# Hybrid encoder block on one core: first norm and w_in in two halves, the last modulation column in the V pass, the query weight loaded by k tile

## The chip, the core and the metric

The kernel runs on one core of a Trainium2 chip. Its engines are TensorE (PE: matmuls; PEld is its weight load), VectorE (DVE), ScalarE (ACT) and GpSimd (POOL). SyncE (SP) issues most of the loads. The metric is the time of one execution in microseconds, as the device measures it. All data are float32 in HBM.

## The reference

```python
c_act = jax.nn.silu(c)
mod = c_act @ ada_w[l] + ada_b[l]                 # 2048 x 12288 weight: 100 MB
shift1, scale1, gate1, shift2, scale2, gate2 = jnp.split(mod, 6, axis=-1)
h = modulate(rms_norm(x, pre_mix_g[l]), shift1, scale1)
proj = h @ w_in[l]                                # 2048 -> 1856: pool | q latent | kv latent | rope key
y_pool = multiscale_pool(proj[..., :o1], pool_w[l], pool_scale[l])
y_mla = mla_attention(proj[..., o1:o2], ...)      # 8 heads, low-rank q and kv, rotary part
y = jnp.concatenate([y_pool, y_mla], axis=-1) @ w_out[l]
x = x + gate1[:, None, :] * rms_norm(y, post_mix_g[l])
h = modulate(rms_norm(x, pre_ffn_g[l]), shift2, scale2)
y = peer_ffn(h, peer_wq[l], peer_sub_keys[l], peer_u[l], peer_v[l])   # 16384 experts
x = x + gate2[:, None, :] * rms_norm(y, post_ffn_g[l])
```

Sequence 256, model width 2048, one layer.

## The kernel before

**Stages.** The program is written out by hand, engine by engine, with semaphores between them. In order of time: the first norm and its modulation (0 to 111 us), w_in (to 202), the latent projections and the pooling mixer (to 256), attention over 8 heads (to 315), w_out (to 412), second norm, the query weight wq (443 to 551), all 16384 experts' u rows (128 tiles, to 1316), a scatter of the gates (to 1430), all v rows (128 tiles, to 2130), and the tail.

**Float32 products.** Each large product is made of three matmuls of a rounded high part and a low part (the three lines of `split3`, L591 to L593). ACT rounds a weight pair (two k tiles) to `win_high`, `wout_high` or `wq_high` (`weight_high`, L937), DVE makes the low part in place (`weight_low`, L1237). `win_high` has three buffers, so ACT and DVE are at most three pairs ahead of PE. The weights w_uq, w_ukv and pool_w are used as plain float32 (L586).

**The modulation** is no matmul over 2048 but a sum on DVE. `ada_w` is cut into six parts of 2048 columns; a part comes in 8 pieces of 2 MB, and DVE takes 4 steps for a piece: `acc = piece * c_act[:, k] + acc` over 1024 columns (L1227 for the first, L1229 for the others; `ada(n)` is n such steps, 32 to a part). After 32 steps `ada_columns` on PE sums over the partitions into a column of `ps` (L568, 32 instructions), and `scale_column`, `shift_column` or `gate_column` finish it. Gates also go through `gate_rows` (PE), `gate_out` (ACT) and a store to DRAM, from which GpSimd loads them as rows. Steps stand in DVE's queue wherever the author put them, between the other work; a step waits for its piece.

**The ring.** Weights and pieces share six slots of 2 MB, filled by SP strictly in the order of `load_order()`. A load waits until the one six places before it is released:

```python
if kind == "ada":
    return ada_op, i * STEPS + 4 * h + 4
if kind in WEIGHTS:
    return w_used, pair_no(kind, i, 4 * h + 3) + 1
return {"uq": (qpe_mm, 2), "ukv": (v_mm, 4), "pool": (pool_mm, 8), "keys": (key_mm, 4)}[kind]
```

So a piece is released by DVE's fourth step on it, a weight block by PE's last pair of it, the two halves of w_uq by the second rope-query group (`qpe_mm`), w_ukv by the last value group (`v_mm` 4), and pool_w by the last pooling group (`pool_mm` 8).

**Between w_in and attention.** PE makes the queries and the rope queries from the latents `cT`, then the keys, then for each of four pooling groups g two products that wait for `z_ready` g+1 (DVE's `pool_group(g)`, running sums over `uT`), then the values, then it transposes the rotated queries (`k_roped`, `q_roped` from DVE's `rotate`). The first score matmuls follow, and DVE's `maxima(0)` (L1413) opens the softmax chain of the heads.

**u and v passes.** In a v tile ACT rounds two halves of 128x1024 (L1175), DVE makes their low parts (L1667), PE multiplies.

## Time and profile before

| | |
|---|---|
| time, median of 3 runs | 2152.22 us (2151.8 to 2155.94) |
| the profiled execution's own time | 2155.08 us |
| its span, first to last instruction | 2152.3 us |
| PE busy / DVE busy | 1946.9 us (90%) / 1520.1 us (71%) |
| mean granted TensorE clock | 0.96 |
| chain that ended last: PE / DVE / DMA / issue | 79% / 10% / 3% / 3% |

The span is shorter than the time by 2.8 us, which lies before the first and behind the last instruction. PE carries most of the chain that ended last, but not in the first 111 us, where it is busy for 23.7 us.

### The profile page before, as it was taken

The page shows a single profiled execution, that of the slowest core. Times are in us where ns is not written, and L with a number is a line of the kernel's source. Part 1 is how long each engine was busy: PE and PEld are TensorE (multiplying, and loading weights), DVE is VectorE, ACT ScalarE, POOL GpSimd, SP SyncE. Part 2 cuts the span into 40 slices and gives each one's busy share as a digit, 9 for nine tenths or more (in the row PEclk, how much of TensorE's full clock was granted, in tenths as well). Part 3 has the DMA queues.
Part 4 walks back from the last instruction along what each step waited for, and adds up shares of the span by engine and source line. Part 5 has one row for each costly group of instructions (what it writes and reads, how often), then busy time and mean ns, then how long its engine had stood idle before and what let it go on. Part 6 is the DMA issues. An engine that isn't in the chain of part 4 may idle for free.

```text
span 2152.3 us, 37807 instructions
## 1 busy us (share of the span) xinstructions
PE 1946.9 (90%) x12388; PEld 1757.5 (82%) x12388; DVE 1520.1 (71%) x2136; ACT 898.1 (42%) x1311; POOL 432.6 (20%) x290
## 2 busy tenths in 40 slices
PE   0489989798999999999999997679999999999995
PEld 0479658698999999999999997568888888888884
DVE  6897489775689999999976667975555555555554
ACT  1143233453334444444444445654444444444443
POOL 1000020000234444444444446840000000000001
PEclk9799859899999999999999999999999999999998
DMA  9989469979567676666677771045555555555553
GB/s 392 414 306 353 157 246 367 295 227 268 131 168 183 180 184 182 180 182 176 175 186 180 184 183 59 0 134 192 192 194 195 194 190 192 194 195 192 190 193 117
DMA packets 227889, 436.99 MB, mean 203 GB/s; under 512 B 23106, under 2 KB 157696, under 8 KB 214016
## 3 DMA queue, kind: packets, MB, share of 16 engines
q1 hardware_dynamic: 226240, 427.84, 63.9%
q0 software_dynamic: 1536, 8.48, 1.0%
q8 instruction: 30, 0.49, 0.1%
q14 instruction: 19, 0.16, 0.0%
q10 hardware_dynamic: 64, 0.02, 0.0%
HBM read 432.04 MB, written 4.21 MB: 203 GB/s over the span
## 4 chain that ended last, share of the span: by engine, by line
PE 79%; DVE 10%; DMA 3%; issue 3%; ACT 2%; DVEq 1%; SPq 1%; POOL 0%; ACTq 0%; POOLq 0%
PE ps L591 14%; PE ps L592 14%; PE ps L593 14%; PE ps L877 11%; PE ps L878 11%; PE ps L880 11%; DVE acc L1229 3%; DVE hotB L1636 2%; DMA ring<-in_ada_w_dram 2%; PE ps L586 2%; DMA i<-consts_dram 1%; DVEq L1636 1%; DVE ring_low L1237 1%; PE ps L568 1%; PE ps L703 1%
## 5 line engine op out<-in xcount | busy, mean ns | idle before, releaser
L591 PE MATMUL ps<-h2H,eH 128*128 128x256 f32 x2048 | 581.5, 284 | 5.8 <-DVE eL L1584 4.5
L592 PE MATMUL ps<-h2L,eH 128*128 128x256 f32 x2048 | 581.0, 284 | 0.0
L593 PE MATMUL ps<-h2H,eL 128*128 128x256 f32 x2048 | 580.9, 284 | 0.0
L1667 DVE TENSOR_TENSOR eL<-raw,eH 128x1024 fp32r<-128x1024 f32 x256 | 313.6, 1225 | 338.2 <-ACT eH L1175 338.2
L1175 ACT CAST eH<-raw 128x1024 fp32r<-128x1024 f32 x256 | 269.9, 1055 | 385.4 <-PE ps L880 379.8
L496 POOL TENSOR_TENSOR eL<-raw,eH 128x1024 fp32r<-128x1024 f32 x128 | 311.4, 2433 | 572.9 <-ACT eH L1101 572.9
L877 PE MATMUL ps<-eH,aH 128*128 128x512 f32 x1024 | 399.2, 390 | 3.6 <-DVE eL L1667 3.6
L591 PEld LDWEIGHTS ps<-h2H,eH 128*128 128x128 f32 x2048 | 394.6, 193 | 6.7 <-DVE eL L1584 5.2
L878 PE MATMUL ps<-eL,aH 128*128 128x512 f32 x1024 | 398.9, 390 | 0.0
L593 PEld LDWEIGHTS ps<-h2H,eL 128*128 128x128 f32 x2048 | 394.7, 193 | 0.0
L592 PEld LDWEIGHTS ps<-h2L,eH 128*128 128x128 f32 x2048 | 394.6, 193 | 0.0
L1593 DVE STREAM_TRANSPOSE raw<-raw 128x1024 f32<-128x1024 f32 x256 | 317.4, 1243 | 87.2 <-DMA raw<-in_peer_u_dram 79.0
L1101 ACT CAST eH<-raw 128x1024 fp32r<-128x1024 f32 x256 | 267.2, 1045 | 199.6 <-PE ps L593 160.1
L880 PE MATMUL ps<-eH,aL 128*128 128x512 f32 x1024 | 315.7, 389 | 0.0
L1229 DVE SCALAR_TENSOR_TENSOR acc<-ring,c_act,acc 128x1024 f32<-128x1024 f32 x180 | 227.1, 1295 | 23.1 <-DMA ring<-in_ada_w_dram 20.9
L877 PEld LDWEIGHTS ps<-eH,aH 128*128 128x128 f32 x1024 | 192.7, 188 | 43.8 <-issue 3.7
L880 PEld LDWEIGHTS ps<-eH,aL 128*128 128x128 f32 x1024 | 192.5, 188 | 40.1
L878 PEld LDWEIGHTS ps<-eL,aH 128*128 128x128 f32 x1024 | 192.6, 188 | 39.9
L1584 DVE TENSOR_TENSOR eL<-raw,eH 128x1024 fp32r<-128x1024 f32 x128 | 155.9, 1218 | 39.1 <-ACT eH L1101 38.5
L350 POOL TENSOR_TENSOR result<-x,scaled 128x2048 f32<-128x2048 f32 x1 | 4.5, 4474 | 712.7 <-DVEq L1687 712.7
L1116 ACT ACTIVATE acts<-ps 128x256 f32 (+1 forms) x128 | 49.2, 384 | 225.0 <-PE ps L593 225.0
L591 PE MATMUL ps<-h2H,wq_high 128*128 128x256 f32 x256 | 76.2, 297 | 13.6 <-DVE ring_low L1237 11.5
(254 smaller groups left out, 2313.1 us busy)
## 6 DMA issues: line engine op xcount, KB each, us to landing
raw<-in_peer_u_dram SPq DMA_DIRECT2D x1024, 128.0 KB, 3.0
raw<-in_peer_v_dram SPq DMA_DIRECT2D x256, 512.0 KB, 3.4
ring<-in_ada_w_dram SPq DMA_DIRECT2D x48, 2048.0 KB, 19.9
ring<-in_w_out_dram SPq DMA_DIRECT2D x8, 2048.0 KB, 11.9
ring<-in_peer_wq_dram SPq DMA_DIRECT2D x32, 512.0 KB, 15.5
ring<-in_w_in_dram SPq DMA_DIRECT2D x6, 2048.0 KB, 14.7
ring<-in_w_uq_dram SPq DMA_DIRECT2D x2, 1536.0 KB, 9.0
ring<-in_w_in_dram SPq DMA_DIRECT2D x2, 1280.0 KB, 11.7
```

Of the source, the lines that this page charges most:

```text
L496: pool.tensor_tensor(by_k(eL[:, j % RING, :]), turned(raw[:, j % RAW, :]), by_k(eH[:, j % RING, :].bitcast(F32)), ALU.subtract).then_inc(u ...
L591: pe.matmul(o, lh, rh, start=start, stop=False, skip_group_check=True)
L592: pe.matmul(o, lh, rl, start=False, stop=False, skip_group_check=True)
L593: return pe.matmul(o, ll, rh, start=False, stop=stop, skip_group_check=True)
L877: pe.matmul(o[n], lh, vh[n], start=start, stop=False, skip_group_check=True)
L878: pe.matmul(o[n], lh, vl[n], start=False, stop=False, skip_group_check=True)
L880: mm = pe.matmul(o[n], ll, vh[n], start=False, stop=stop, skip_group_check=True)
L1101: act.copy(by_k(eH[:, j % RING, :]), turned(raw[:, j % RAW, :])).then_inc(u_hi, 1)
L1175: act.copy(eH[:, slot, :], raw[:, slot, :]).then_inc(v_hi, 1)
L1229: ins = dve.scalar_tensor_tensor(a, w, c_act[:, k:k + 1], a, ALU.mult, ALU.add)
L1593: dve.transpose(raw[:, j % RAW, :], raw[:, j % RAW, :]).then_inc(u_tr, 1)
L1667: dve.tensor_tensor(eL[:, slot, :], raw[:, slot, :], eH[:, slot, :].bitcast(F32), ALU.subtract).then_inc(v_lo, 1)
```

## The change

1. **Modulation parts 0 and 1** are cut another way: part 0 is now the first 1024 columns of shift1 and of scale1 together, part 1 the second 1024 of both. A piece of them comes in two loads of 1 MB. The first norm's modulation and w_in are done in two halves of 8 k tiles: PE runs the low half of all four column blocks n = 2, 3, 0, 1, with `ada_columns(1)` ahead of the last of them, then the high half of all four. x is loaded after the first piece, and the constants from ACT's queue.
2. **Positions of steps.** DVE takes 34 steps ahead of the first modulation (64 before), then 30 in the low half, 12 in the high half, 28 between w_in and attention (6 before), 18 in attention as before, 38 in w_out (40), none in wq (32).
3. **The rope angles** (`angles()`) move from the start to the last column block of w_in's high half, ahead of the diagonal matrices `diag` and `tmpr` that PE's latent transposes wait for (`lat_diag`).
4. **Gate 1:** `ada_columns(2)` and `gate_rows(0)` move from the projections to the start of w_out.
5. **Gate 2** (part 5, 16.8 MB) leaves the ring and the wq stage. It comes as 16 pieces of 1 MB in the v pass, the first three from SP, the others from GpSimd's queue; DVE takes one step a tile in tiles 3 to 34, then a transpose, a reduction and two row operations. `ada_columns(5)`, `gate_rows(1)` and `gate_out(1)` around the first u round are gone.
6. **wq** is loaded with 8 loads of 256 KB over 128 partitions for a block, before with 4 loads of 512 KB over 32 partitions each.

```diff
-PARTS = (1, 0, 2, 3, 4, 5)
+PARTS = (None, None, 2, 3, 4, 5)
...
-    win = [("win", n, h) for n in WIN_ORDER for h in range(2)]
     wout = [("wout", n, h) for n in range(4) for h in range(2)]
     wq = [("wq", n, h) for n in range(4) for h in range(2)]
-    between = ([("uq", 0, 0), ("ada", 3, 0), ("uq", 1, 0), ("ada", 3, 1), ("ukv", 0, 0), ("pool", 0, 0)]
-               + [("ada", 3, p) for p in range(2, PIECES)])
-    return ([("ada", 0, p) for p in range(PIECES)] + [("ada", 1, p) for p in range(PIECES)] + mixed(win, 2)
-            + between + mixed(wout, 4) + mixed(wq, 5) + [("keys", 0, 0)])
+    low, step = [], 0
+    for n, count in zip(WIN_ORDER, (3, 3, 1, 1)):
+        low += [("win", n, 0)] + [("ada", 1, step + p) for p in range(count)]
+        step += count
+    high = [("win", n, 1) for n in WIN_ORDER]
+    between = ([("ada", 2, 0), ("ada", 2, 1), ("uq", 0, 0), ("ada", 2, 2), ("uq", 1, 0), ("ada", 2, 3), ("ukv", 0, 0),
+                ("pool", 0, 0)] + [("ada", 2, p) for p in range(4, PIECES)] + [("ada", 3, p) for p in range(PIECES)])
+    return ([("ada", 0, p) for p in range(PIECES)] + low + high
+            + between + mixed(wout, 4) + wq + [("keys", 0, 0)])
...
-        per_slot[n % SLOTS] += 64 if key[0] == "wq" else 16
+        per_slot[n % SLOTS] += 128 if key[0] == "wq" else 32 if key[0] == "ada" and key[1] < 2 else 16
...
+        def load_piece(eng, k):
+            eng.dma_start(piece[k % 3][:], ada_v[:, k, 5 * D:6 * D]).then_inc(piece_done(k)[0], 16)
...
+                if kind == "ada" and i < 2:
+                    for k in range(2):
+                        sp.dma_start(dst[:, k * D:(k + 1) * D].rearrange("p (m n) -> p m n", m=2),
+                                     ada_v[:, 2 * h + k, 0:2 * D].rearrange("p (m n) -> p m n", m=2)
+                                     [:, :, i * 1024:(i + 1) * 1024]).then_inc(done, 16)
+                elif kind == "ada":
...
-                    for q in range(4):
-                        sp.dma_start(wide(kind, i, 8 * h)[q * QUAD:(q + 1) * QUAD],
-                                     wq_v[q, :, ks, i * W:(i + 1) * W]).then_inc(done, 16)
+                    for k in range(8):
+                        sp.dma_start(wide(kind, i, 8 * h)[:, k, :],
+                                     wq_v[8 * h + k, :, :, i * W:(i + 1) * W]).then_inc(done, 16)
...
+            sp.wait_ge(u_used, 2 * TILES)
+            for k in range(3):
+                load_piece(sp, k)
...
+            for k in range(3, KT):
+                pool.wait_ge(piece_step, 2 * (k - 2))
+                load_piece(pool, k)
...
-            ada_columns(1, 0)
-
-
-            for n in WIN_ORDER:
-                if n == 1:
-                    pe.wait_ge(lat_out, 2)
-                for k in range(KT):
-                    if n == 2 and k % 2 == 0:
+            ada_columns(0, 0, 0)
+
+            def win_half(n, half):
+
...
+            for n in (2, 3, 0):
+                win_half(n, 0)
+            ada_columns(1, 7, HI_COLS, False)
+            win_half(1, 0)
+
+
+            for n in WIN_ORDER:
+                win_half(n, 1)
                 if n == 0:
                     pe.wait_ge(lat_diag, 4)
...
-            pe.wait_ge(u_out, 8)
             for tt in range(TT):
                 mm_group(ps[:, 4 + tt, :], lambda k: cT[:, k, tt * P:(tt + 1) * P],
                          lambda k: wuq[k // 2][:, k % 2, :, NOPE:NOPE + ROPE], 4).then_inc(qpe_mm, 1)
-            ada_columns(2, 0)
...
-            gate_rows(0, 1)
-
             pe.wait_ge(k_roped, 1)
             pe.wait_ge(q_roped, 1)
-            pe.wait_ge(grow_out, 1)
+            pe.wait_ge(u_out, 8)
...
+            ada_columns(2, 0, 2 * KT)
             for n in range(4):
                 for k in range(KT):
+                    if n == 0 and k == 8:
+                        gate_rows(0, 1)
...
-            ada_columns(5, 3)
             for i in range(ROUND):
                 u_tile(0, i, i < 3)
-            gate_rows(1, 3)
...
-            gate_out(1, 3)
...
+            def input_columns(i, bank, first):
+
+                dve.wait_ge(acc_used, 2 * i + 2)
+                cols = slice(8 * i, 8 * i + 8)
+                dve.tensor_tensor(mod1[:, 1, cols], ps[:, bank, first:first + 8], vcols[:, V_B0 + 8 * i:V_B0 + 8 * i + 8],
+                                  ALU.add)
+                seq(dve.scalar_tensor_tensor(mod1[:, 0, cols], ps[:, bank, first + 8:first + 16], 1.0,
+                                             vcols[:, V_B1 + 8 * i:V_B1 + 8 * i + 8], ALU.add, ALU.add))
+                dve.nop().then_inc(mod_read, 1)
+                seq(dve.tensor_tensor(mod1[:, 0, cols], mod1[:, 0, cols], vcols[:, V_G1 + 8 * i:V_G1 + 8 * i + 8], ALU.mult))
...
+            def inputs(half):
+
+                k0 = 8 * half
+                for k in range(k0, k0 + 4):
+                    modulate(k)
+                if half:
+                    weight_low("win", 1, 2)
+                h_low(k0 // 2)
+                modulate(k0 + 4)
+                modulate(k0 + 5)
+                if half:
+                    weight_low("win", 1, 3)
+                else:
+                    weight_low("win", 2, 0)
+                h_low(k0 // 2 + 1)
+                modulate(k0 + 6)
+                modulate(k0 + 7)
+                h_low(k0 // 2 + 2)
+                weight_low("win", 2, 4 if half else 1)
+                h_low(k0 // 2 + 3)
...
+            ada(10)
...
+            ada(18)
+            ada(2)
+            input_columns(0, 0, 0)
             dve.wait_ge(xn_out, KT)
-
-            def modulate(k):
-                dve.tensor_scalar(hT[:, k, :], hT[:, k, :], mod1[:, 0, k:k + 1], mod1[:, 1, k:k + 1],
-                                  ALU.mult, ALU.add).then_inc(h_f, 1)
-
-            def h_low(j):
-                dve.wait_ge(h_hi, j + 1)
-                h = slice(2 * j, 2 * j + 2)
-                dve.tensor_tensor(hL[:, h, :], hT[:, h, :], hH[:, h, :].bitcast(F32), ALU.subtract).then_inc(h_lo, 1)
-
-            for k in range(4):
-                modulate(k)
-            for j in range(2, KT // 2):
-                modulate(2 * j)
-                modulate(2 * j + 1)
-                h_low(j - 2)
-                if j == 3:
-                    weight_low("win", 2, 0)
-            h_low(KT // 2 - 2)
-            weight_low("win", 2, 1)
-            h_low(KT // 2 - 1)
-
+            inputs(0)
             for n in WIN_ORDER:
-                for j in range(8):
-                    if n == 0 and j == 5:
+                for j in range(4):
+                    if (n, j) in ((2, 0), (2, 1), (1, 2), (1, 3)):
+                        continue
+                    weight_low("win", n, j)
+                    ada({2: 2, 3: 3, 0: 3, 1: 1}[n])
+            input_columns(1, 7, HI_COLS)
+            inputs(1)
+            for n in WIN_ORDER:
+                for j in range(4, 8):
+                    if n != 2 or j >= 5:
+                        weight_low("win", n, j)
+                    if n == 0 and j == 7:
...
+                    if n == 1 and j == 5:
                         dve.wait_ge(lat_sq, 3)
...
-                    ada(1)
-            dve.wait_ge(trig_ready, 2)
-
+                    if n < 2:
+                        ada(2 - n)
+                    if n == 1 and j == 4:
+                        angles()
...
+            ada(6)
+            dve.wait_ge(trig_ready, 2)
...
+            ada(4)
...
-            gate_column(0, 2, 0, V_B2, V_PO1)
-            ada(6)
+            ada(18)
...
-                    ada(2 if j % 4 == 3 else 1)
+                    ada(2 if j == 3 or (n < 2 and j == 7) else 1)
+                    if n == 0 and j == 2:
+                        gate_column(0, 2, 0, V_B2, V_PO1)
...
-                    ada(1)
...
-            gate_column(1, 5, 3, V_B5, V_PO2)
...
-            with dve.Fori(1, TILES // 3) as r:
+            def last_gate(step):
+
+                k, h = step // 2, step % 2
+                if h == 0:
+                    dve.wait_ge(*piece_done(k))
+                a, w = (t[:, h * 1024:(h + 1) * 1024] for t in (sums2, piece[k % 3]))
+                if k == 0:
+                    dve.tensor_scalar(a, w, c_act[:, 0:1], None, ALU.mult).then_inc(piece_step, 1)
+                else:
+                    dve.wait_ge(piece_step, step - 1)
+                    dve.scalar_tensor_tensor(a, w, c_act[:, k:k + 1], a, ALU.mult, ALU.add).then_inc(piece_step, 1)
+
+            def gate_row(i, op):
+                dve.wait_ge(gate2_in, 16)
+                dve.wait_ge(extra_in, 16 * (i + 1))
+                dve.tensor_tensor(gate2[:], gate2[:], extra[:], op).then_inc(gate2_ready, 1)
+
+            for tile in range(3, 36):
+                v_tile(tile, tile % 3, False)
+                if tile < 35:
+                    last_gate(tile - 3)
+            dve.wait_ge(piece_step, 2 * KT)
+            dve.transpose(sums2[:], sums2[:]).then_inc(sums_turned, 1)
```

How the change moves instructions is shown at three places. First SP's queue (the ring's loads; `ring_49` to `ring_54` are the six slots, and what a row waits for stands at its end) around w_ukv. Before:

```order
L386 DMA ring_51<-in_w_uq_dram 128x2x1536 [waits w_used]
L379 DMA ring_52<-in_ada_w_dram 128x2x2048 [waits ada_op]
L386 DMA ring_53<-in_w_uq_dram 128x2x1536 [waits w_used]
L379 DMA ring_54<-in_ada_w_dram 128x2x2048 [waits ada_op]
L392 DMA ring_49<-in_w_ukv_dram 128x2x2048 [waits w_used]
L389 DMA ring_50<-in_pool_w_dram 128x8x256 [waits ada_op]
L379 DMA ring_51<-in_ada_w_dram 128x2x2048 [waits qpe_mm]
```

Of the change:

```order
L410 DMA ring_53<-in_w_uq_dram 128x2x1536 [waits w_used]
L403 DMA ring_54<-in_ada_w_dram 128x2x2048 [waits w_used]
L416 DMA ring_49<-in_w_ukv_dram 128x2x2048 [waits ada_op]
L413 DMA ring_50<-in_pool_w_dram 128x8x256 [waits ada_op]
L403 DMA ring_51<-in_ada_w_dram 128x2x2048 [waits qpe_mm]
L403 DMA ring_52<-in_ada_w_dram 128x2x2048 [waits ada_op]
L403 DMA ring_53<-in_ada_w_dram 128x2x2048 [waits qpe_mm]
L403 DMA ring_54<-in_ada_w_dram 128x2x2048 [waits ada_op]
L403 DMA ring_49<-in_ada_w_dram 128x2x2048 [waits v_mm]
L403 DMA ring_50<-in_ada_w_dram 128x2x2048 [waits pool_mm]
```

The positions behind w_ukv wait for the same events as before; the pieces that stand there are now 4 to 7 of part 2 and 0 and 1 of part 3, and before they were 2 to 7 of part 3. Second, DVE's queue ahead of the first row of the softmax chain (`s_sb<-ps,mask`; the `acc` rows are modulation steps, `zT` the end of the last pooling group). Before:

```order
L1383 TENSOR_TENSOR zT<-catT,uT 128x16
L1251 TENSOR_TENSOR gcol<-ps,vcols 128x16
L1253 TENSOR_TENSOR gcol<-gcol,vcols 128x16
L1227 TENSOR_SCALAR acc_105<-ring_52,c_act 128x1024
L1227 TENSOR_SCALAR acc_106<-ring_52,c_act 128x1024
L1229 SCALAR_TENSOR_TENSOR acc_105<-ring_52,c_act,acc_105 128x1024
L1229 SCALAR_TENSOR_TENSOR acc_106<-ring_52,c_act,acc_106 128x1024
L1229 SCALAR_TENSOR_TENSOR acc_105<-ring_54,c_act,acc_105 128x1024
L1229 SCALAR_TENSOR_TENSOR acc_106<-ring_54,c_act,acc_106 128x1024
L1413 SCALAR_TENSOR_TENSOR s_sb<-ps,mask 128x384
```

Of the change (eight more steps, on `ring_52` to `ring_54`, stand between `zT` and the first of these rows):

```order
L1296 SCALAR_TENSOR_TENSOR acc_103<-ring_54,c_act,acc_103 128x1024
L1296 SCALAR_TENSOR_TENSOR acc_104<-ring_54,c_act,acc_104 128x1024
L1294 TENSOR_SCALAR acc_105<-ring_49,c_act 128x1024
L1294 TENSOR_SCALAR acc_106<-ring_49,c_act 128x1024
L1296 SCALAR_TENSOR_TENSOR acc_105<-ring_49,c_act,acc_105 128x1024
L1296 SCALAR_TENSOR_TENSOR acc_106<-ring_49,c_act,acc_106 128x1024
L1296 SCALAR_TENSOR_TENSOR acc_105<-ring_50,c_act,acc_105 128x1024
L1296 SCALAR_TENSOR_TENSOR acc_106<-ring_50,c_act,acc_106 128x1024
L1296 SCALAR_TENSOR_TENSOR acc_105<-ring_50,c_act,acc_105 128x1024
L1296 SCALAR_TENSOR_TENSOR acc_106<-ring_50,c_act,acc_106 128x1024
L1510 SCALAR_TENSOR_TENSOR s_sb<-ps,mask 128x384
```

The last eight steps ahead of the softmax chain read `ring_49` and `ring_50`, the two slots whose loads wait for `v_mm` and `pool_mm` above. Third, DVE's queue at the end of w_in's block n = 0, where the diagonal matrices are made. Before:

```order
L1237 TENSOR_TENSOR ring_low_57<-ring_51,win_high_140 128x1024
L1344 TENSOR_SCALAR diag<-cst,stat 128x128
L1346 TENSOR_SCALAR tmpr<-cst,stat 128x128
L1344 TENSOR_SCALAR diag<-cst,stat 128x128
L1346 TENSOR_SCALAR tmpr<-cst,stat 128x128
L1229 SCALAR_TENSOR_TENSOR acc_104<-ring_52,c_act,acc_104 128x1024
```

Of the change (eight more rows of the angles and a step stand ahead of these, and ahead of them the low part of n = 1's first pair):

```order
L1360 TENSOR_SCALAR ang<-ang 128x64
L1361 TENSOR_SCALAR ang<-ang 128x64
L1362 TENSOR_TENSOR ang<-ang 128x64
L1363 TENSOR_SCALAR ang<-ang 128x64
L1304 TENSOR_TENSOR ring_low_60<-ring_54,win_high_140 128x1024
L1438 TENSOR_SCALAR diag<-cst,stat 128x128
L1440 TENSOR_SCALAR tmpr<-cst,stat 128x128
L1438 TENSOR_SCALAR diag<-cst,stat 128x128
L1440 TENSOR_SCALAR tmpr<-cst,stat 128x128
```

The diagonal matrices have moved behind two low parts of the next block, three steps and the angles.

## Rows read from the trace of the kernel before

**Rows 1.** Window: us, busy PE, PEld, DVE, ACT, POOL; clock; DMA share, GB/s

```profile
0.00:111.00 111.00, 23.69 (x130) 23.11 (x131) 84.42 (x97) 15.99 (x31) 7.40 (x18) 0.86 1.00 403
```

**Rows 2.** Timeline up to w_in: start, length, instructions, wait before

```profile
10.50 1.42 DVE L1227 TENSOR_SCALAR acc<-ring,c_act 128x1024 f32<-128x1024 f32 x2 [10.50 <-DMA ring<-in_ada_w_dram]
...
97.42 6.96 PE L568 MATMUL ps<-cst,acc 128*128 128x1 f32 x32 [21.74 <-DVE acc L1229]
...
111.02 0.76 PE L591 MATMUL ps<-win_high,hH 128*128 128x512 f32 x1 [6.64 <-DVE ring_low L1237]
...
118.12 1.41 DVE L1227 TENSOR_SCALAR acc<-ring,c_act 128x1024 f32<-128x1024 f32 x2
```

**Rows 3.** Timeline of DVE in w_in

```profile
125.24 1.28 DVE L1229 SCALAR_TENSOR_TENSOR acc<-ring,c_act,acc 128x1024 f32<-128x1024 f32 x1
126.44 1.22 DVE L1237 TENSOR_TENSOR ring_low<-ring,win_high 128x1024 fp32r<-128x1024 f32 x1
...
134.25 0.83 DVE L1237 TENSOR_TENSOR ring_low<-ring,win_high 128x640 fp32r<-128x640 f32 x1
```

**Rows 4.** Chain that ended last through w_in: start, length, what

```profile
117.75 0.52 PE ps L591
...
121.63 0.23 PE ps L591
...
138.72 0.24 PE ps L593
...
153.73 0.38 PE ps L591
...
176.60 2.68 PE ps L580 x24
...
201.93 1.58 ACT cT L984 x4
```

**Rows 5.** Windows of DVE: angles; diagonals; key rotation, group 2; query rotation, group 3

```profile
31.70:34.90 3.20, 2.73 (x13) 1.00 1.03 430
171.00:172.70 1.70, 1.22 (x5) 1.00 0.99 388
203.10:210.80 7.70, 6.66 (x25) 1.00 0.94 349
224.60:235.50 10.90, 9.91 (x25) 0.69 0.52 194
```

**Rows 6.** Timeline of PE: pooling groups, then values

```profile
238.23 7.07 PE L586 MATMUL ps<-zT,ring 128*128 128x256 f32 x32
245.14 7.03 PE L586 MATMUL ps<-ring,cT 128*128 128x512 f32 x16
```

**Rows 7.** SP's timeline, and DMA issues at 224 to 226 us with landing time

```profile
224.59 38.98 SPq L379 DMA_DIRECT2D ring<-in_ada_w_dram  x6
...
ring<-in_ada_w_dram SPq DMA_DIRECT2D x1, 2048.0 KB, 8.6
```

**Rows 8.** Timelines of DVE and PE: first softmax row; first w_out matmul

```profile
258.19 0.56 DVE L1413 SCALAR_TENSOR_TENSOR s_sb<-ps,mask 128x384 f32<-128x384 f32 x1 [15.76 <-PE ps L703]
...
315.46 0.79 PE L591 MATMUL ps<-wout_high,catH_a 128*128 128x512 f32 x1
```

**Rows 9.** Groups in wq, 443 to 551 us: busy, mean ns, idle before

```profile
L591 PE MATMUL ps<-h2H,wq_high 128*128 128x256 f32 x240 | 71.6, 298 | 13.6 <-DVE ring_low L1237 11.5 <-ACT qT L1083 2.1
```

**Rows 10.** Start of u pass: timelines of DVE, PE; waits, 545 to 620 us

```profile
561.54 1.23 DVE L1584 TENSOR_TENSOR eL<-raw,eH 128x1024 fp32r<-128x1024 f32 x1 [12.45 <-ACT eH L1101]
...
565.05 0.46 PE L591 MATMUL ps<-h2H,eH 128*128 128x256 f32 x1
...
PE ps L591 <- DVE eL L1584: 3.4, 1, 3.4
```

**Rows 11.** The v pass: a group of the page; landing of the v loads

```profile
L1667 DVE TENSOR_TENSOR eL<-raw,eH 128x1024 fp32r<-128x1024 f32 x256 | 313.6, 1225 | 338.2 <-ACT eH L1175 338.2
...
DMA to landing us min/median/max: 2.9/3.4/6.7
```

More of the change, by code:

```diff
@@ L60 @@
 V_B2 = P
-V_B5 = V_B2 + KT
-V_PO1 = V_B5 + KT
-V_PO2 = V_PO1 + KT
-V_ALL = V_PO2 + KT
+V_PO1 = V_B2 + KT
+V_ALL = V_PO1 + KT
 TWO_PI_A = 6.28125
@@ L209, in hybrid_block @@
     gate2 = at("gate2", M + 4096, [D])
+    piece = [at(f"piece{i}", M + 2048 * i, [D]) for i in range(3)]
+    sums2 = at("sums2", M + 6144, [D])
+    quarter = at("quarter", S + 1712, [KT * 4])
+    quarters = at("quarters", M + 6144, [4, KT * 4])
+    half2 = at("half2", M + 6400, [3, KT * 4])
+    extra = at("extra", M + 6144, [D])
     raw = at("raw", M + 8192, [RAW, HF])
@@ L605, in _ @@
                      lambda tt: diag[:, tt, :])
-            ada_columns(1, 0)
-            for n in WIN_ORDER:
-                if n == 1:
-                    pe.wait_ge(lat_out, 2)
-                for k in range(KT):
-                    if n == 2 and k % 2 == 0:
+            ada_columns(0, 0, 0)
+            def win_half(n, half):
+                for k in range(8 * half, 8 * half + 8):
+                    if n == WIN_ORDER[0] and k % 2 == 0:
                         pe.wait_ge(h_lo, k // 2 + 1)
@@ L1051, in _ @@
                         weight_high("wout", n, j)
+                    if n == 0 and j == 6:
+                        gate_out(0, 1)
                     if n and j == 2:
@@ new lines, in _ @@
+            dve.wait_ge(silu_done, 1)
+            ada(10)
+            dve.wait_ge(vec_t, 2)
+            seq(dve.tensor_copy(vcols[:], ps[:, 1, 0:V_ALL]))
+            dve.nop().then_inc(vec_cols, 1)
+            ada(2)
+            dve.wait_ge(x_sq, 1)
+            inverse_mean(stat[:, 2:4], stat[:, 0:2], D)
+            dve.nop().then_inc(x_rs, 1)
+            ada(2)
+            dve.wait_ge(cst_in, 16)
+            dve.wait_ge(x_rs, 2)
+            for tt in range(TT):
+                seq(dve.tensor_scalar(diag[:, tt, :], ident, stat[:, 4 + tt:5 + tt], None, ALU.mult))
+                dve.nop().then_inc(diag1, 1)
@@ L1671, in _ @@
                 v_tile(j, j, True)
-            with dve.Fori(1, TILES // 3) as r:
+            def last_gate(step):
[18 more added lines that the diff above has]
+            dve.transpose(sums2[:], sums2[:]).then_inc(sums_turned, 1)
+            for tile in range(36, 39):
+                v_tile(tile, tile % 3, False)
+            dve.wait_ge(sums_turned, 1)
+            dve.tensor_reduce(quarter[:], sums2[:].rearrange("p (b l) -> p b l", l=QUAD), AX_X,
+                              ALU.add).then_inc(quarter_ready, 1)
+            with dve.Fori(13, 30) as r:
+                for j in range(3):
+                    v_tile(r * 3 + j, j, False)
+            gate_row(0, ALU.add)
+            with dve.Fori(30, 35) as r:
+                for j in range(3):
+                    v_tile(r * 3 + j, j, False)
+            gate_row(1, ALU.mult)
+            with dve.Fori(35, TILES // 3) as r:
                 for j in range(3):
```

200 lines of the change are left out of this document (108 added, 92 removed).

## The prediction

> **What bounds the kernel now.** I read the windows of the stages first. In the first 111 us PE is busy for 23.7 us, while DMA runs at share 1.00 and 403 GB/s and DVE is busy for 84.4 us [rows 1]: the loads of the modulation weight and DVE's sums of them bound this stage together, PE waits. Then I read the chain that ended last and the timelines behind it. From w_in on the chain is PE's; w_in takes from 111.0 to 201.9 us [rows 2, 4]. Between w_in and attention PE is still the chain, and DVE is early for it: it waits 15.8 us for the first scores [rows 8]. Attention is a chain of short DVE, ACT and PE work. In wq PE loses 13.6 us to waits [rows 9], because DVE has modulation steps in its queue whose pieces are late. The u and v passes are PE's; in the v pass DVE waits for ACT's rounding (338.2 us over 256 roundings) [rows 11].
>
> So there are four places to cost: the front, the way from w_in to attention, the entry of w_out, and wq with the start of u. Times below are on the clock of the profile before; E is the end of w_in's matmuls, 201.9 before [rows 4].
>
> **1. The front.** A 2 MB piece costs 2.1 MB / 403 GB/s = 5.2 us of DMA [rows 1]. The first lands at 10.3 us as now [rows 2]; x and the other seven of part 0 follow, so the last lands at 10.3 + 8 x 5.2 = 51.9. Four steps at 1.2 us (from one start to the next [rows 3]) end at 56.8, the 32 column matmuls take 7.0 [rows 2], so the first modulation starts near 64, where it was 104.4. PE's first w_in matmul followed 6.6 us behind (104.4 to 111.0) [rows 2]; here 5 to 6, so near 69: 42 us early.
>
> This is given back in the low half, which holds 30 steps. DVE: the norm's half with its first two low parts takes about 8 us (13.7 us for all 16 k tiles, 104.4 to 118.1, of which 2.4 are low parts, so 5.7 + 2.4 [rows 2, 3]); it ends at 72.4. Two pairs of n = 2 with two steps each are 7.2 (low part 1.2, step 1.2), four of n = 3 with three steps each 4 x (0.8 + 3.6) = 17.7: 97.3. Now n = 0 needs its weight block. Its load stands behind two pieces of part 1, the first of which goes into the slot of w_in's block (2, low), which PE releases at 82 (69 + 48 matmuls at 0.23, and 1.9 for a slow clock, below). One lone piece lands 8.6 us after its issue [rows 7], the next two loads 5.2 us each: 101.0, and about a low part's 1.2 for ACT's rounding: 102. DVE goes on with 4 x 4.8 = 19.2 for n = 0 and 4.8 for n = 1: part 1 is summed at 126.
>
> The second half of the column matmuls costs up to 3.5 (half of 7.0): 129.5. PE then has everything else in front of it: halves of 11.3 (n = 1: 179.3 to 201.9), 11.0 (n = 2: 48 matmuls at 0.23), 7.5 (n = 3: 138.7 to 153.7) and 11.4 (n = 0: 153.7 to 176.6) [rows 4]. In n = 0's high half a pair costs DVE 1.2 + 2.4 = 3.6 us, PE 2.9; with three pairs of buffer that costs PE some 1.2. PE is at the latent transposes at 129.5 + 11.3 + 11.0 + 7.5 + 11.4 + 1.2 = 171.9. They wait for the diagonal matrices, and DVE, done with n = 0's last low part at 169.6, has before them two steps, a low part, a step, the angles (3.2), a low part and the matrices (1.7) [rows 5]: with 0.3 for the small statistics 11.2, so 180.8. PE stands for 9 us, a wait that is not there now. Then 2.7 for the transposes [rows 4], 11.3 for n = 1, and the clock: after a pause matmuls of 512 columns take 0.43 us for 3.9 us before they take 0.23 (117.75 to 121.63) [rows 4], a loss of 1.9. E = 180.8 + 2.7 + 11.3 + 1.9 = 196.7: **-5.2 us**. The bounds: -12 if the loads run ahead of this and the wait for the matrices is halved, +2 if pieces in two loads with rows of half the length move at a tenth less than 403 GB/s.
>
> **2. From w_in to attention.** DVE has 28 steps here, 6 before, and they stand in front of work that PE waits for. Steps 76 to 79 read piece 3 of part 2, released by E; that wait (E + 8.6, done E + 13.5) hides. Steps 80 and 81 read piece 4, whose load waits for the rope queries, E + 22.7 (224.6 less 201.9) [rows 7]; it lands at E + 31.3, the steps end at E + 33.7. Behind them in DVE's queue stand the key rotation and pooling group 2, 7.7: E + 41.4 (before: done at 210.8, E + 8.9). Four steps, 4.8: E + 46.2. Query rotation and group 3, 10.9 [rows 5]: E + 57.1 (before E + 33.6). PE waits for it, then takes a quarter of 7.07 for the last pooling group and 7.03 for the values [rows 6], and 1.9 for the slow clock: E + 67.8. Only then is w_ukv's slot free, and piece 0 of part 3 is loaded into it: E + 76.4, piece 1 one load later: E + 81.6. The last eight of the 18 steps need these two, so DVE is free at E + 86.4 and opens attention there. Before it did so at 258.2 - 201.9 = E + 56.3 [rows 8], waiting for PE. **+30.1 us**; with -5.2 the first softmax row comes at 283. Bounds: +26 if the clock does not fall and the pieces land in 7 us, +34 if both are worse. The attention loop itself keeps its two steps a head and its length.
>
> The Trainium skill (DMA: Bandwidth & Descriptors, Anatomy of one DMA) gives a DMA 2.0 us and the bytes at 436 GB/s, an estimate of 6.8 us for 2 MB against the 8.6 of the row. By it the two lone loads on this way would be 1.8 us shorter each, and the term would be 26.5. I keep the row: it is the same load on the same queue in this kernel.
>
> **3. Entry of w_out.** The 32 column matmuls of gate 1 now stand between the last head and w_out's first matmul at 315.5 [rows 8], where nothing covers them: 7.0 at the slow clock [rows 2]. The steps are long done. **+7.0**; at least 3.5, if the clock is up. What they cost where they stood is in term 2, whose chain no longer goes through PE.
>
> **4. wq and start of u.** Of 11.5 us for low parts in wq [rows 9] some 2 stay, for rounding the stage's first pair; the rest is DVE held by steps and their late pieces. **-9.5**, down to -11.5, up to -6 if one of the new loads is late. The first u matmul (565.1) stood behind the column matmuls of part 5; without them the next limit is the first low part at 561.5 + 1.2 = 562.8 [rows 10]: -2.3. The pause of 3.4 us at the first u round's end [rows 10], when ACT waited for the gate's row, goes, with the 1.9 of slow clock behind it: -5.3. Together **-7.6**.
>
> **5. The v pass** gets 32 steps of 1.28 us [rows 3]. DVE idles 338.2 / 256 = 1.32 us before each rounding [rows 11], so a step between two tiles fits; the transpose and row operations use the slack of the three buffers. The 16.8 MB go beside v loads that land in 3.4 us [rows 11]. **0**, up to +41 (32 x 1.28) if every step delayed PE.
>
> **Sum.** -5.2 + 30.1 + 7.0 - 9.5 - 7.6 + 0 = +14.8 us. Against the profiled execution's 2155.1 that is 2169.9; it stood 2.9 above the median of its runs, so against the median 2167.0. I say 2167.
>
> **The rivals.**
> A (forecast, 0.66): the front's 42 us are used up by the low half, the late diagonals and the steps ahead of attention. Ends at 2155 to 2182.
> B (0.13), **faster**: the front keeps its gain. If the low half is held by neither loads nor steps, w_in ends at 69 + 90.9 (111.0 to 201.9) + 3.5 = 163; the sum is then -18.9, or 2133. It decides at E = 181.9, where the sum is zero. For it speaks that PE starts 42 us early; against it that 30 steps and 12 more low parts, 36 + 12 us, must pass DVE behind 72, so that part 1 is not there before 120 even if no load is late.
> C (0.10), **no change**: the front ends some 10 us earlier than I say and the lone loads land as quickly as the first bound, so that terms 1 and 2 sum to about 10: 2152.
> D (0.06), **slower still**: the v pass pays for a good part of its steps, or the new loads of parts 0 and 1 are slow; with half of the 41 us: 2188.
> E (0.05): wq does not gain, because its waits move to the new loads: +9.5, 2177, inside my range.
>
> **Numbers.** A change of 0.2% (4.3 us) is about what a measurement of this kernel can tell. Faster by more: B and a part of C, 0.15. Within: 0.10. Slower: 0.75. The range reaches from 2150 (C's lower side) to 2181.
>
> **What would show it.** First w_in matmul near 69; part 1's last step near 126; a PE pause of some 9 us at the latent transposes; w_in's end near 197; pauses of PE for `zT` of groups 2 and 3; the load of part 3's first piece issued after the values; the first softmax row near 283; PE column matmuls of 7 us before w_out; no wait of DVE for `ada_w` in wq, and wq's matmuls some 9 us shorter; no pause after the first u round; a v pass of 700 us. It is wrong if the steps between w_in and attention do not wait for their pieces, or if w_in ends before 182.

## The result, and the profile after

The changed kernel takes 2216.65 us (median of 4 runs, 2215.42 to 2218.32), the kernel before 2152.01 us in the runs beside it. The ratio is 1.0298, with a 95% interval of 1.028 to 1.0316: 64.6 us slower. I had forecast 2167, with 2181 as the upper end: the sign was right, the size was four times what I said, and it lies outside the range.

The profiled execution took 2215.42 us, its span is 2213.6 us, 61.3 more than before. The page, its slices and its chain (the slices are 55 us each; they answer to what the table on the profile before gives):

```profile
PE 1955.4 (88%) x12355; PEld 1763.3 (80%) x12355; DVE 1526.4 (69%) x2141; ACT 897.7 (41%) x1311; POOL 443.6 (20%) x311
...
PE   1688469976799999999999998669999999999995
...
DMA  9983588632456666666676775017876755565553
GB/s 383 369 310 139 238 327 318 234 132 103 127 143 184 180 184 181 182 183 177 176 185 179 182 183 159 0 38 267 289 269 188 247 191 191 195 206 197 196 191 114
...
PE 72%; DVE 11%; DMA 6%; SPq 5%; issue 3%; ACT 2%; DVEq 1%; POOL 0%; ACTq 0%; POOLq 0%
```

PE is busy 8.5 us longer than before, so nearly all of the loss is waiting. SPq, SyncE's instruction queue, had 1% of the chain before and now has 5%, and in slices 9 to 11 (443 to 609 us, the wq stage) only 103 to 132 GB/s are moved. The chain, in order of time, shows how it gets there; the second line is E, the end of w_in (beside [rows 4]), the third the last steps ahead of attention:

```profile
180.94 4.31 PE ps L627 x24
196.58 1.58 ACT cT L1054 x4
...
275.83 2.55 DVE acc L1296 x3
...
337.60 6.62 PE ps L615 x32
...
444.91 2.44 SPq L420
447.40 2.44 SPq L420
449.88 2.44 SPq L420
...
475.52 13.66 DMA ring<-in_peer_wq_dram
489.20 3.89 ACT wq_high L989 x4
...
537.48 13.66 DMA ring<-in_peer_wq_dram
...
609.57 1.20 ACT qT L1154 x4
...
1708.14 17.05 DMA raw<-in_peer_v_dram
```

Through wq the chain does not run over PE but over the issues of wq's loads (L420): each of them holds SP for 2.5 us. The groups of wq's matmuls and of its rounding, and the DMA view of 467 to 590 us:

```profile
L638 PE MATMUL ps<-h2H,wq_high x256: 281/281/582, 466.3 to 609.0; 128*128 128x256 f32 x128
```
```profile
L638 PE MATMUL ps<-h2H,wq_high 128*128 128x256 f32 x256 | 79.1, 309 | 38.0 <-DVE ring_low L1304 36.8 <-ACT qT L1154 1.2
L989 ACT CAST wq_high<-ring 128x1024 fp32r<-128x1024 f32 x32 | 31.3, 1043 | 93.8 <-DMA ring<-in_peer_wq_dram 90.3 <-PE ps L640 3.4
```
```profile
DMA  2222222222222222222222222222222222222289
GB/s 102 101 103 107 101 103 101 101 103 107 102 103 101 102 103 101 102 108 102 103 101 101 103 101 101 109 102 101 103 101 102 103 101 102 103 107 102 103 217 202
```

PE waits 36.8 us for low parts, where it was 11.5 [rows 9]; DVE no longer has steps there, but ACT waits 90.3 us for the loads: 7.6 to 16.9 us ahead of each of the last six of the eight blocks. Those loads run at 102 GB/s with the 16 DMA engines busy for two tenths only. The stage has the bandwidth and does not use it. The matmuls themselves are slower too, 309 ns each where the mean was 297 over all of wq (298 in [rows 9], which begin at 443 us and leave out the first 16); the mean granted clock is 0.86 over wq's matmuls, and 0.92 in the kernel before.

By stages, both profiled executions, from the first row of one stage to that of the next (w_out's first matmul is at 315.5 before [rows 8] and 344.1 after; wq's first at 437.2 and 466.3, its last starts at 550.1 and 609.0; v's matmuls start from 1432.3 to 2129.4 and from 1482.7 to 2189.3):

| stage | before | after | difference | forecast |
|---|---|---|---|---|
| to E | 201.9 | 196.6 | -5.3 | -5.2 |
| E to the first softmax row | 56.3 | 84.0 | +27.7 | +30.1 |
| to w_out's first matmul | 57.3 | 63.5 | +6.2 | +7.0 |
| to wq's first matmul | 121.7 | 122.2 | +0.5 | 0 |
| wq's matmuls | 112.9 | 142.7 | **+29.8** | **-9.5** |
| to v's first matmul | 882.2 | 873.7 | -8.5 | -7.6 |
| v's matmuls | 697.1 | 706.6 | +9.5 | 0 |
| to the end of the span | 22.9 | 24.3 | +1.4 | 0 |

Two terms failed: wq by 39 us, v by 9.5.

### The profile page after: what moved, and what is told of

Read it like the earlier page. It is cut to its first block, busy times and chain, and to the rows that moved or that the text cites. A ratio compares the mean times of both kernels' runs of the same rounds, so it can differ in the third digit from the quotient of the medians.

```text
span 2213.6 us, 37648 instructions
## 1 busy us (share of the span) xinstructions
PE 1955.4 (88%) x12355; PEld 1763.3 (80%) x12355; DVE 1526.4 (69%) x2141; ACT 897.7 (41%) x1311; POOL 443.6 (20%) x311
## 4 chain that ended last, share of the span: by engine, by line
PE 72%; DVE 11%; DMA 6%; SPq 5%; issue 3%; ACT 2%; DVEq 1%; POOL 0%; ACTq 0%; POOLq 0%
PE ps L638 12%; PE ps L639 12%; PE ps L640 12%; PE ps L927 10%; PE ps L928 10%; PE ps L930 10%; SPq L420 4%; DVE acc L1296 3%; DMA ring<-in_ada_w_dram 3%; DVE hotB L1733 2%; DMA ring<-in_peer_wq_dram 2%; PE ps L633 1%; DVE ring_low L1304 1%; DMA raw<-in_peer_v_dram 1%; DMA ring<-in_w_in_dram 1%
## 5 line engine op out<-in xcount | busy, mean ns | idle before, releaser
L1296 DVE SCALAR_TENSOR_TENSOR acc<-ring,c_act,acc 128x1024 f32<-128x1024 f32 x150 | 188.0, 1297 | 35.9 <-DMA ring<-in_ada_w_dram 33.1
L638 PE MATMUL ps<-h2H,wq_high 128*128 128x256 f32 x256 | 79.1, 309 | 38.0 <-DVE ring_low L1304 36.8
L1304 DVE TENSOR_TENSOR ring_low<-ring,wq_high 128x1024 fp32r<-128x1024 f32 x32 | 37.2, 1220 | 91.7 <-ACT wq_high L989 91.6
```

The source lines that it names most:

```text
L638: pe.matmul(o, lh, rh, start=start, stop=False, skip_group_check=True)
L1296: ins = dve.scalar_tensor_tensor(a, w, c_act[:, k:k + 1], a, ALU.mult, ALU.add)
```

## The experiments

**1 to 4: the form of wq's loads.** A block was four loads, each of 32 partitions and 8 k tiles; now it is eight, each one k tile of 128 partitions, whose rows lie in HBM as 4 quarters of 32 rows. The first two runs change only this in the changed kernel: back to the old form, and 16 loads of 32 partitions and two k tiles (128 KB).

```diff
-                    for k in range(8):
-                        sp.dma_start(wide(kind, i, 8 * h)[:, k, :],
-                                     wq_v[8 * h + k, :, :, i * W:(i + 1) * W]).then_inc(done, 16)
+                    for k in range(4):
+                        for q in range(4):
+                            sp.dma_start(wide(kind, i, 8 * h)[q * QUAD:(q + 1) * QUAD, 2 * k:2 * k + 2],
+                                         wq_v[q, :, 8 * h + 2 * k:8 * h + 2 * k + 2,
+                                              i * W:(i + 1) * W]).then_inc(done, 16)
```

> The changed kernel with w_q loaded again in four loads of 512 KB a block, each for 32 partitions; ring order and steps stay. Theory S (spread): a load of one k tile, whose DRAM side has an outer size of 4, goes over 4 of the 16 DMA engines, which is why DMA is at share 0.22 and 102 GB/s in wq. Then w_q's matmuls take 142.8 less 39 = 104 us, the kernel is near 2216.7 - 39 = 2178, and the DMA share in wq is near 0.9. Theory W (waits): w_q is slow because its blocks are released late by PE, whatever the form of the loads. Then the time stays within 5 us of 2216.7.

> The changed kernel with w_q in 16 loads of 128 KB a block, each of 32 partitions and two k tiles. Theory S: outer size 32, so all 16 engines: near 2178 as with four loads a block. Theory N (number): each load instruction costs SP some 2.46 us whatever its form. Then a block takes 16 x 2.46 = 39 us instead of 20, the eight blocks 315 instead of 163, and the kernel ends near 2216.7 + 150 = 2367.

The third has as many loads of as many bytes as the second, but each is half a k tile: 64 partitions, two quarters of 32 rows.

```diff
+                    for k in range(8):
+                        for q in (0, 2):
+                            sp.dma_start(wide(kind, i, 8 * h)[q * QUAD:(q + 2) * QUAD, k, :],
+                                         wq_v[8 * h + k, q:q + 2, :, i * W:(i + 1) * W]).then_inc(done, 16)
```

> The changed kernel with w_q in 16 loads of 128 KB a block, each of half a k tile: 64 partitions, outer size 2 on the DRAM side. As many loads of as many bytes, in rows as long, as in the run with pairs of k tiles. Theory S: 2 of 16 engines, so 51 GB/s, 41 us a block, and an end near 2216.7 + 8 x 20.5 = 2380, with a DMA share of 0.12 in wq. Theory N: near 2367, but then the run with pairs is there too. If only the rows or the byte count matter: the same time as the run with pairs, near 2178.

The fourth is the kernel before with only the new form (eight loads of a k tile).

> The kernel before with only the form of w_q's loads changed (eight of 256 KB a block). Theory S: w_q's 16.8 MB need 164 us on four engines and the pieces of the last modulation part some 42 us more; from the first issue at 390 this ends at 596, and w_q's matmuls near 608 instead of 550: near 2152 + 57 = 2209. Theory W: near 2152.

| kernel | time, us | ratio to before, 95% |
|---|---|---|
| old form in the changed kernel | 2167.92 | 1.0051 to 1.0085 |
| 16 loads, 32 partitions x two k tiles | 2167.56 | 1.005 to 1.0084 |
| 16 loads, half a k tile | 2378.76, one run | |
| before, by k tile | 2242.29 | 1.0399 to 1.0434 |

The views of DMA in the third (480 to 520 us) and in the first (467 to 566 us):

```profile
DMA  1101111111111111111111111111111111111111
GB/s 57 61 37 53 49 53 45 49 51 51 49 53 49 51 51 49 53 49 53 66 51 51 51 51 51 49 53 49 51 51 49 53 49 51 51 51 51 51 49 53
```
```profile
DMA  9999996799929995099999000000000000000000
GB/s 228 218 214 216 220 213 127 207 213 221 206 62 251 218 219 113 11 295 256 234 240 220 22 0 7 0 0 0 0 0 0 7 0 0 0 0 7 0 0 0
```

The rate goes with the outer size of the HBM side: 102 GB/s with 4, 51 with 2, and with 32 a share of nine tenths and mostly 210 to 250. It goes neither with the number of loads (128 of them in the second run occupy SP for 82.6 us, 64 in the changed kernel for 162.8) nor with their bytes. Theory S gave 2178, 2178, 2380 and 2209; measured are 2168, 2168, 2379 and 2242. The number of SBUF partitions changes with the form too, but it can't be what counts: the rate halves from 128 partitions to 64 and is highest at 32. W and N are out: W by the first run, N by the second. The first two are 10 us faster than I said; 7 of them lie in wq's matmuls, which take 97.3 us, not 104. In the first run PE waits only 4.5 us there, and a matmul takes 286 ns in the mean, at a mean granted clock of 0.98:

```profile
L638 PE MATMUL ps<-h2H,wq_high 128*128 128x256 f32 x256 | 73.2, 286 | 4.5 <-DVE ring_low L1304 2.4 <-ACT qT L1154 2.1
```

The fourth is 33 us slower than I said. There SP is blocked in turn by a block and by a piece of the last modulation part, 28 us a round and not the 25.8 I took, which makes 18 us over eight rounds. The rows below show one round and the start of the next. Most of the rest lies at the end of the loads: the chain gives 18.6 us from the last issue for wq to its landing. ACT rounds that block at 623.4, where I had the transfers end at 596, and the last matmul starts 15.5 us later, where I had allowed 12. All of the run's loss lies in wq: its span is 88.7 us longer than before, and wq's last matmul starts 88.8 us later (638.9 for 550.1).

```profile
496.30 25.52 SPq L396 DMA_DIRECT2D ring<-in_peer_wq_dram  x8
521.86 2.43 SPq L379 DMA_DIRECT2D ring<-in_ada_w_dram  x1
524.33 26.72 SPq L396 DMA_DIRECT2D ring<-in_peer_wq_dram  x8
```

All further kernels have the old form (2167.92 is their base) and undo one more thing each. They ran in other groups of runs than the base; the kernel before, run beside each group, took 2152.8, 2152.5 and 2152.8 us, so their times can be set beside each other.

**5: gate 2's row.** GpSimd stores the row in HBM as 2048 single floats; here it stores 32 runs of 256 bytes, and DVE reads it back permuted.

```diff
-            pool.dma_start(gate_dram[1].rearrange("(b l) -> l b", l=QUAD), half2[0:QUAD, 2, :],
-                           allow_slow_non_contiguous=True).then_inc(row2_stored, 16)
+            pool.dma_start(gate_dram[1].rearrange("(l b) -> l b", l=QUAD), half2[0:QUAD, 2, :]).then_inc(row2_stored, 16)
...
+                    dve.tensor_tensor(extra[:].rearrange("p (b l) -> p b l", l=QUAD),
+                                      gate2[:].rearrange("p (l b) -> p b l", l=QUAD),
+                                      extra[:].rearrange("p (b l) -> p b l", l=QUAD), op).then_inc(gate2_ready, 1)
```

> The changed kernel with w_q's loads in the old form (near 2167.9), and gate 2's row stored to DRAM in 32 runs of 256 bytes instead of 2048 elements of 4 bytes; DVE reads it back in permuted order when it adds the bias. In the v pass PE stood 6.4 us once and ran slow after it, behind v loads that took 16 us, while this store was under way. Theory E (elements): the store of single elements fills the DMA engines for some 10 us. Then the pause goes, the v pass is 700 us again and the kernel near 2158.5. Theory X: the 2 MB of x1 and two rows spread over 128 partitions, 4 MB that are loaded at the same place, delay the v loads. Then it stays near 2168.

Measured: 2166.86 us, ratio 1.0051 to 1.0099, not to be told from the base. The landing time of the store and the longest wait of ACT for a v load, first in the base, then here:

```profile
gate_dram<-half POOLq DMA_DIRECT2D x1, 8.0 KB, 9.6
```
```profile
1672.18 1.04 ACT L1245 CAST eH<-raw 128x1024 fp32r<-128x1024 f32 x1 [10.03 <-DMA raw<-in_peer_v_dram]
```
```profile
gate_dram<-half POOLq DMA_DIRECT2D x1, 8.0 KB, 2.8
```
```profile
1666.36 1.06 ACT L1244 CAST eH<-raw 128x1024 fp32r<-128x1024 f32 x1 [5.21 <-DMA raw<-in_peer_v_dram]
```

The wait is halved, and v's matmuls span 701.3 us instead of 705.1 in the traces. That is more than scatter: in the five other kernels with the same v pass as the base (experiments 2, 3 and 7 to 9) they span 704.4 to 705.1 us, and 706.6 in the changed kernel. So E is a part, and something else is left, which the next run takes up.

**6: tail loads one by one,** on top of the fifth. The row, the bias row, and x1 in two halves are each loaded when the one before has landed.

```diff
-            pool.dma_start(x1[:], x1_dram.rearrange("t p d -> p t d")).then_inc(tail_in, 16)
...
+            pool.wait_ge(gate2_in, 16)
...
+                    pool.wait_ge(extra_in, 16)
+                    for tt in range(TT):
+                        pool.dma_start(x1[:, tt, :], x1_dram[tt]).then_inc(tail_in, 16)
+                        pool.wait_ge(tail_in, 16 * (tt + 1))
```

> The kernel with w_q's loads in the old form and gate 2's row in runs of 256 bytes (2166.9), and now gate 2's row, its bias row and the two halves of x1 are loaded one behind the other, each when the one before has landed, instead of 4 MB at once. With the row in runs the v pass, from its first to its last matmul, was 701.3 us in the trace, 4.2 more than before the change. Theory X (burst): v loads queue behind 4 MB, 10 us of DMA, where three buffers of 2.7 us give them less. 1 MB at a time costs 2.6 us and fits. Then the v pass is 697 to 698 us and the kernel near 2161 to 2163. Rival: the rest comes from the 32 steps or from the 1 MB pieces; then it stays at 701 and near 2167.

Measured: 2161.99 us (1.0032 to 1.0072), with v's matmuls at 699.0 us in the trace. Theory X has the time, 1 us more in v than it gave. With both mends the v pass costs 2 us more than before in this trace, and 0.5 and 0.8 us more in those of the tenth and eleventh kernel (697.6 and 697.9), the 32 steps included.

**7: steps behind the groups.**

```diff
             pool_group(1, WINDOWS[1])
-            ada(6)
...
             pool_group(2, WINDOWS[2])
-            ada(4)
...
             pool_group(3, WINDOWS[3])
-            ada(18)
+            ada(28)
```

> As the kernel with w_q's loads in the old form (near 2167.9), with the 6 and 4 steps that stand ahead of pooling groups 2 and 3 in DVE's queue moved behind group 3 (28 steps in one piece there). Theory Q (queue): PE waits for groups behind steps whose pieces are late, and w_ukv's slot and so the first piece of part 3 come late. Then the values end near E+50 instead of E+68, that piece lands near E+59, DVE opens attention near E+69 instead of E+84: -15, near 2153. Theory D (the DMA and DVE have no room): the 28 steps and their seven pieces need the time wherever they stand; the first softmax row stays within 4 us of E+84, near 2166.

Measured: 2152.51 us (0.9988 to 1.0013), 15.4 below the base. The first softmax row comes at 265.9, 66.2 behind this run's E of 199.7. PE's waits for `zT` are gone; in the changed kernel they were these (PE alone, the second row at the transposes of experiment 8):

```profile
PE ps L633 <- DVEq L1479: 19.2, 2, 12.0
PE ps L627 <- DVEq L1441: 8.7, 1, 8.7
```

Theory Q. The same 28 steps and seven pieces are done 18 us sooner behind E, so neither DVE nor DMA was short.

**8: matrices first.** Three steps and the angles go behind the diagonal matrices.

```diff
-                    if n < 2:
-                        ada(2 - n)
-                    if n == 1 and j == 4:
-                        angles()
+                    if n == 0 and j < 7:
+                        ada(2)
+                    if n == 1 and j > 4:
+                        ada(2)
+                    if n == 1 and j == 5:
+                        angles()
```

> As the kernel with w_q's loads in the old form (near 2167.9), with three of the steps and the angles, which stood ahead of the diagonal matrices in DVE's queue, moved behind them. My account: PE's pause of 8.7 us at the latent transposes shrinks by 2.4 + 1.2 + 3.2 = 6.8 and everything behind moves with it: E near 190, 2161. If instead the stretch up to attention is set by the transfers of pieces, which do not wait for this, E is earlier but the first softmax row is not: 2168.

Measured: 2161.93 us (1.003 to 1.0065), 6.0 below the base. PE's pause is 2.6 instead of 8.7 us, E is 191.3, and the first softmax row comes at 275.1, E + 83.8 as ever:

```profile
PE ps L627 <- DVEq L1441: 2.6, 1, 2.6
```

**9: gate 1's columns** right behind the first two scores.

```diff
             scores(1)
+            ada_columns(2, 0, 2 * KT)
             pe.wait_ge(v_out, 4)
...
-            ada_columns(2, 0, 2 * KT)
             for n in range(4):
```

> As the kernel with w_q's loads in the old form (near 2167.9), with gate 1's 32 column matmuls issued right behind the scores of heads 0 and 1, where PE waits for the first softmax, instead of between attention and w_out. My account: they are hidden there: -6.6, near 2161. Rival: they delay the first probabilities' transposes, since part 2's sum is late: 2168.

Measured: 2163.89 us (1.0035 to 1.0073), 4.0 below the base. In the trace the way from the first softmax row to w_out's first matmul is 57.3 us instead of 63.5, as before the change; E was 199.9 in this execution against 198.0 in the base's. Whether that explains the 2 us that the median lacks, one profile each can't say.

**10 and 11: all mends together, and the kernel before with gate 2 alone.** The tenth has experiments 1 and 5 to 9 at once. The eleventh is the kernel before with the parts of the change that concern gate 2 (and experiments 5 and 6), and nothing of the new front, steps, gate 1 or wq loads:

```diff
-            + between + mixed(wout, 4) + mixed(wq, 5) + [("keys", 0, 0)])
+            + between + mixed(wout, 4) + wq + [("keys", 0, 0)])
...
-                    ada(1)
...
-            ada_columns(5, 3)
...
-            gate_rows(1, 3)
```

> All mends in one: w_q's old loads, row in runs and tail loads one by one, steps behind the groups, matrices first, column matmuls behind the first scores. From 2167.9: -15.4, -6.0, -4 to -6.6 and -6 to -8 add up if the mechanisms are independent: 2132 to 2137. If they share their slack (DVE or the transfers of pieces bound the way to w_out whatever the order), some of it does not come: 2145.

> The kernel before, front and projections untouched, with only gate 2's part moved from w_q and u into the v pass (with the row in runs and the tail loads one by one, w_q's loads as they were). Account by stages from the traces: w_q's matmuls 113.4 us become 97.5 as in the mended kernel (-15.9), the way from w_q's end to the first v matmul 881.9 becomes 873.2 (-8.7), the v pass 697 stays, the end +1.5: -23, near 2129.5. If the steps in w_q were covered after all, it stays near 2150. Beside the combined kernel it tells what the new front and order of steps bring when mended: with 2129.5 and 2134 nothing or less.

Measured: 2130.37 us (0.9883 to 0.992) and 2132.0 us (0.9892 to 0.9928). One by one the mends gave -15.4, -6.0, -4.0 and -5.9, which makes 2136.6; together they give 6.2 us more, 1.6 below the range I had put on record. By stages the traces agree: beside the base the tenth is 6.5 us shorter to E, 18.2 from E to the first softmax row (the same as experiment 7), 6.2 to w_out's first matmul (as experiment 9) and 7.5 in v's matmuls. A part of what was missing when they ran alone lay elsewhere in those executions: E came 1.7 and 1.9 us later in experiments 7 and 9 than in the base, though nothing ahead of it had changed. Both are 21 to 22 us faster than the kernel before, and they don't differ by more than their runs scatter. First lines of the rows of `s_sb` and of wq's matmuls, tenth and eleventh:

```profile
L1513 DVE SCALAR_TENSOR_TENSOR s_sb<-ps,mask x8: 552/557/559, 257.7 to 304.3; 128x384 f32<-128x384 f32 x8
...
L641 PE MATMUL ps<-h2H,wq_high x256: 281/281/415, 437.0 to 534.3; 128*128 128x256 f32 x128
```
```profile
L1454 DVE SCALAR_TENSOR_TENSOR s_sb<-ps,mask x8: 547/558/558, 257.3 to 304.1; 128x384 f32<-128x384 f32 x8
...
L636 PE MATMUL ps<-h2H,wq_high x256: 281/281/388, 437.3 to 532.2; 128*128 128x256 f32 x128
```

Attention opens at 257.7 with the new front and at 257.3 with the old one (258.2 before [rows 8]). So the front in halves, with its first matmul 42 us early, brings nothing by the time attention starts, even with its waits mended: w_in ends 11.3 us earlier in the tenth (191.5 for 202.8), and the 28 steps behind it, where the eleventh has 6, use that up. By attention both orders have done about the same number of steps, 104 and 102. Whether another division of the steps would keep the 11 us was not run. The whole gain is gate 2's: beside the kernel before, the eleventh is 18.0 us shorter in wq's matmuls (94.9 us), 8.2 from there to v's first matmul, and 2.5 longer behind that.

## Why the prediction was right and wrong

**1. The front: right in each step.** First w_in matmul at 69.28 (69), the low part of n = 0 at 102.37 (102), end of w_in 196.6 (196.7), a PE pause of 8.7 us (9). Experiment 8 shows its cause. Rival B, a front that keeps its 42 us, did not come. The windows tell why, here of the tenth kernel up to 126 us and of the kernel before over w_in (window, its length, busy PE, PEld, DVE, ACT and POOL, clock, DMA share, GB/s):

```profile
0.00:69.00 69.00, 16.96 (x98) 16.42 (x98) 44.09 (x50) 15.32 (x29) 6.44 (x16) 0.86 1.00 389
69.00:126.00 57.00, 39.99 (x210) 35.48 (x211) 51.87 (x49) 13.14 (x15) 0.00 (x0) 0.83 0.97 368
```
```profile
111.00:202.00 91.00, 88.50 (x600) 82.50 (x600) 82.59 (x96) 37.08 (x53) 0.00 (x0) 0.96 0.88 340
```

DMA is at a share of 1.00 and 0.97 up to 126 us, and DVE is busy for 51.9 of the 57 us behind 69. The changed kernel has the same shares and 51.7 us. PE starts early and then runs at the pace of the loads and steps that it used to stand behind; it is busy for 40 of 57 us (38 in the changed kernel).

**2. From w_in to attention: right** (+27.7 for +30.1). Pieces landed and groups ended where I put them within some 2 us (group 2 at E + 40.2 for 41.4, group 3 at E + 55.9 for 57.1, part 3's first piece at E + 74.3 for 76.4); experiment 7 shows the mechanism, which is the order of DVE's queue, not the amount of work. The two lone loads took 7.4 and 8.0 us from issue to landing, between the 8.6 of the row and the 6.8 worked out from the page; the section that the prediction cites for it gives its formula for DMAs issued from GpSimd, and these come from SP.

**3. Entry of w_out: right** (+6.2 for +7.0), by experiment 9.

**4. wq: this step was wrong.** I wrote that of the 11.5 us for low parts some 2 stay and the rest goes, -9.5, "up to -6 if one of the new loads is late". The mechanism of that half is shown, but its size was too small: with the old form wq's matmuls take 15.6 us less than before, beyond the -11.5 of my bound. The waits give 9.1 of them (4.5 for 13.6); I had counted nothing else. The other 6.5 are the matmuls, 286 ns each for 297, at a mean granted clock of 0.98 for 0.92. What failed is that the sum puts the new form of the loads at nothing, without a reason. The bound stands for one late load; all eight blocks take 20.6 us (2.1 MB at 102 GB/s), and ACT waits for the last six of them. In the old form the eight blocks hold SP for 76.2 us, 9.5 a block. By rival E the waits would move to the new loads, and I gave this 0.05 and priced it at the mere loss of the gain. It is that mechanism at a higher price: wq does not merely lose its gain but takes 29.8 us more than before. Between the two forms lie 45.4 us of wq (97.3 and 142.7) and 48.7 us of the time (2167.92 and 2216.65). The rows before held no load of this shape, so the price had to be bounded from both sides, and I left the upper side out.

The rate follows the outer dimension of the HBM side: 102 GB/s for 4 and 51 for 2, half of it. The Trainium skill (DMA: Bandwidth & Descriptors, Why a DMA increments its semaphore by 16 and not by 1) has the rule: a copy runs on k engines of 16, with k the largest number up to 16 that divides the outermost sizes of both access patterns. By it these loads get 4 and 2, the old ones 16. The runs agree: shares of two tenths and of one tenth. The prediction used that page for the time of a lone load and left this rule out.

**5. Start of u: right** (-8.5 for -7.6). **The v pass: +9.5, not 0.** I had bounded it by +41, from DVE's steps; but the steps are hidden, as I said. The cost came from what I had called row operations that "use the slack of the three buffers": the loads that feed them. 8 KB in single floats take 9.6 us to land; the 2 MB of x1 are issued right behind them, and 2 MB of rows as soon as they have landed. ACT then waits 10.8 us for a v load (10.0 in the base), and PE 6.4. Experiments 5 and 6 take 6 of the 8 us back.

Without the form of wq's loads the change is worth 2167.9, where I had 2167.0. That this is so near owes something to luck: v was 8 us dearer than I said and wq 6 us cheaper.

## What to carry to other kernels

Price a load by its access pattern as well as by its bytes: look at the outermost size on both sides, and if the profile has no load of that shape, take the slowest case as a bound of its own. An early start is worth only what the loads and the other engines behind it let through; count them to the point where both orders have done the same work. A move that frees a queue (gate 2 out of wq) can be worth all of a change, so time its parts alone before the whole is judged.

## What the runs showed that I had not expected

- wq's loads of 32 partitions in rows of 2 KB run at 210 to 250 GB/s with the DMA share at nine tenths, little more than half of the 403 GB/s that the pieces of the modulation weight, with rows of 8 KB, reach at a share of 1.00 [rows 1]. Whether the length of the rows makes the difference was not tested.
- Loads on few engines hold the queue that issues them: an issue takes SP 2.5 us through most of wq, with 256 KB on 4 engines and with 128 KB on 2 alike, which is 64 KB an engine in both. In the kernel before with loads by k tile (experiment 4) a piece of another tensor, which can use all 16 engines, lands 18.9 us after its issue, against 8.6 for a lone one [rows 7].
